# Two transformer layers written out in place of a loop, with the last weight splits and gating laid between residual sums

## The reference, cut to what matters

```python
for l in range(DEPTH):
    x = x + 0.5 * swiglu(rmsnorm(x, ffn1_norm[l]), ffn1_w_gate[l], ffn1_w_up[l], ffn1_w_down[l])
    h = rmsnorm(x, mix_norm[l])
    ... = jnp.split(h @ w_in[l], split_at, axis=-1)      # three kinds of attention
    x = x + o @ w_out[l]
    x = x + 0.5 * swiglu(rmsnorm(x, ffn2_norm[l]), ffn2_w_gate[l], ffn2_w_up[l], ffn2_w_down[l])
```

## Time and profile before

| | us |
|---|---|
| median of 3 runs | 3130.5 (3124.9 to 3131.53) |
| profiled execution | 3123.23 |
| its span | 3121.4 |
| PE busy | 2920.3 (94%) |
| DVE busy | 1825.3 (58%) |
| ACT busy | 1121.3 (36%) |

### The profile page before, as it was taken

How to read it: one execution, slowest core, us unless ns; L and a number is a source line. 1 busy time by engine, 2 the same in 40 slices (tenths; PEclk the granted TensorE clock), 3 DMA queues, 4 the chain that set the end, 5 groups by cost and what they waited for, 6 DMA issues and landing times.

```text
span 3121.4 us, 36929 instructions
## 1 busy us (share of the span) xinstructions
PE 2920.3 (94%) x13194; PEld 2256.0 (72%) x13194; DVE 1825.3 (58%) x2653; ACT 1121.3 (36%) x1638; POOL 212.4 (7%) x68
## 2 busy tenths in 40 slices
PE   5999999999999998999999999999998999878995
PEld 3888877566688877888777566688876767566774
DVE  4556553675555655565544674566556645469775
ACT  3211132467322223221131566312114333356664
POOL 0000000000000000000000000000000000037663
PEclk8999999999999999999999999999999989989998
DMA  7322332100232322232232000323214212368895
GB/s 161 108 94 84 102 76 67 31 1 25 89 110 84 108 81 95 81 108 94 79 87 52 21 1 24 121 81 108 94 40 108 79 41 81 142 236 315 322 331 195
DMA packets 234685, 324.56 MB, mean 104 GB/s; under 512 B 58720, under 2 KB 202088, under 8 KB 222144
## 3 DMA queue, kind: packets, MB, share of 16 engines
q1 hardware_dynamic: 228400, 309.88, 30.4%
q0 software_dynamic: 5584, 11.02, 1.3%
q10 hardware_dynamic: 576, 2.10, 0.2%
HBM read 317.20 MB, written 14.16 MB: 106 GB/s over the span
## 4 chain that ended last, share of the span: by engine, by line
PE 83%; DVE 4%; DMA 3%; issue 2%; ACT 2%; POOL 2%; DVEq 1%; SPq 1%; ACTq 0%; POOLq 0%
PE score L909 10%; PE score L911 10%; PE score L910 10%; PE acc L1271 8%; PE acc L962 6%; PE acc L940 5%; PE acc L942 5%; PE acc L941 5%; PE score L996 4%; PE acc L1017 4%; PE score L1444 3%; POOL xd_lo L2750 2%; PE acc L1444 2%; PE acc L954 2%; DMA weights<-in_ffn_w_gate 1%
## 5 line engine op out<-in xcount | busy, mean ns | idle before, releaser
L2066 DVE SCALAR_TENSOR_TENSOR x_T<-acc,x_T 128x512 f32<-128x512 f32 x352 | 242.4, 691 | 402.8 <-PE acc L942 402.4
L909 PE MATMUL score<-h_hi,gate_hi 128*128 128x512 f32 x704 | 277.7, 394 | 22.1 <-DVE h_lo L2019 14.1
L910 PE MATMUL score<-h_lo,gate_hi 128*128 128x512 f32 x704 | 275.9, 392 | 0.0
L911 PE MATMUL score<-h_hi,gate_lo 128*128 128x512 f32 x704 | 275.9, 392 | 0.0
L909 PE MATMUL score<-h_hi,up_hi 128*128 128x512 f32 x704 | 275.6, 391 | 0.0
L911 PE MATMUL score<-h_hi,up_lo 128*128 128x512 f32 x704 | 273.9, 389 | 0.0
L910 PE MATMUL score<-h_lo,up_hi 128*128 128x512 f32 x704 | 273.9, 389 | 0.0
L940 PE MATMUL acc<-hid_hi,down_hi 128*128 128x512 f32 x640 | 252.1, 394 | 17.9 <-DVE x_T L2066 17.9
L942 PE MATMUL acc<-hid_hi,down_lo 128*128 128x512 f32 x640 | 251.3, 393 | 0.0
L941 PE MATMUL acc<-hid_lo,down_hi 128*128 128x512 f32 x640 | 251.2, 392 | 0.0
L1620 ACT ACTIVATE exp_tile<-probs 128x512 f32<-128x512 f32 x88 | 50.8, 625 | 409.1 <-DVE probs L2041 409.1
(11 more groups left out here) (437 smaller groups left out, 6350.1 us busy)
## 6 DMA issues: line engine op xcount, KB each, us to landing
weights<-in_ffn_w_gate SPq DMA_DIRECT2D x44, 1024.0 KB, 5.3
weights<-in_ffn_w_up SPq DMA_DIRECT2D x44, 1024.0 KB, 5.4
weights<-in_ffn_w_down SPq DMA_DIRECT2D x44, 1024.0 KB, 5.5
arena<-in_expert_w_gate SPq DMA_DIRECT2D x32, 1024.0 KB, 6.5
arena<-in_expert_w_up SPq DMA_DIRECT2D x32, 1024.0 KB, 6.9
weights<-in_expert_w_down SPq DMA_DIRECT2D x30, 1024.0 KB, 5.9
weights<-in_w_in SPq DMA_DIRECT2D x23, 1024.0 KB, 5.3
weights<-in_w_out SPq DMA_DIRECT2D x8, 768.0 KB, 4.4
```

Source lines behind the costliest of these rows:

```text
L909: mm(ps, hi[:, kc, cols], h_hi[:, kc, :], start=kc == 0, stop=False, skip_group_check=True)
L910: mm(ps, hi[:, kc, cols], h_lo[:, kc, :], start=False, stop=False, skip_group_check=True)
L911: return mm(ps, lo[:, kc, cols], h_hi[:, kc, :], start=False, stop=kc == KC - 1, skip_group_check=True)
L2066: V.scalar_tensor_tensor(x_T[:, c, :], acc[c % 2][:, :], 0.25, x_T[:, c, :], ALU.mult, ALU.add).then_inc(acc_free[c % 2], 1)
```

## The change

It has four parts. (1) The loop over the two layers is written out on all four engines, so that the layer number is a constant; the last low halves of one feed-forward are joined to the next layer (`entering`). (2) At the end of a feed-forward DVE's work is laid out anew: after each of the eight sums of the last but one down product comes one part: for `ph` 1 two halves of the last down weights, then the three steps of `hidden`, then two halves of the next stage's first weights; for `ph` 0 the last down weights are split ahead of all sums, and ACT may split them as soon as the gate half of the last slice has been read. (3) Between the attention's output product and the second feed-forward, ACT splits the first gate weights after the first two chunks of x, and DVE in two halves after the sums of chunks 4 and 5. (4) With layer 1's first gate weights split there, the top of layer 1 has only the last low half left.

```diff
@@ sp, pe, act, dve: the layer loop @@
-            with dve.Fori(0, DEPTH) as l:
-                split_weights(l, 0, 0, 0)
-                for c in range(KC):
-                    low(l, 0, c)
+            for l in range(DEPTH):
+                if l == 0:
+                    split_weights(l, 0, 0, 0)
+                    for c in range(KC):
+                        low(l, 0, c)
+                else:
+                    low(l, 0, KC - 1)
                 add_squares(l * 3, ffn_sq, KC - 1)
...
@@ act @@
-            def enter(k, sq, hi):
+            def enter(k, sq, hi, first_gate=None):
 
                 for c in range(KC):
+                    if first_gate is not None and c == 2:
+                        split_weights(first_gate, 1, 0, 0)
...
-                act.wait_ge(gu_full, gu_at(l, gub, 2 * NSL))
+                act.wait_ge(gu_full, gu_at(l, gub, 2 * NSL - (1 if ph == 0 else 0)))
                 split_weights(l, ph, 2, NSL - 1, tile=ph)
...
                 slices(l, 0)
+                act.wait_ge(gu_full, gu_at(l, 0, 2 * NSL))
                 split_mix(l, 0)
                 enter(l * 3 + 1, mix_sq, mix_h[0])
                 mix(l)
-                split_weights(l, 1, 0, 0)
-                enter(l * 3 + 2, ffn_sq, h_hi)
+                enter(l * 3 + 2, ffn_sq, h_hi, first_gate=l)
                 slices(l, 1)
@@ dve @@
-            def split_weights(l, ph, w, sl, tile=None):
+            def split_weights(l, ph, w, sl, tile=None, half=None):
 
                 tile = w if tile is None else tile
+                cols = slice(0, 2048) if half is None else slice(1024 * half, 1024 * half + 1024)
                 dve.wait_ge(w_hi_ready[w], at(l, 2 * NSL, ph * NSL + sl + 1))
-                V.tensor_tensor(w_lo[tile][:, :], slot[w][:, :], w_hi[tile][:, :], ALU.subtract).then_inc(w_split[w], 1)
+                m = V.tensor_tensor(w_lo[tile][:, cols], slot[w][:, cols], w_hi[tile][:, cols], ALU.subtract)
+                if half != 0:
+                    m.then_inc(w_split[w], 1)
...
+                entering = (l, 1) if ph == 0 else (l + 1, 0) if l + 1 < DEPTH else None
...
                         if last:
                             dve.drain().then_inc(x_final, 1)
-                            if ph == 0 and c >= 1:
-                                low(l, 1, c - 1)
+                            if entering is not None and c >= 1:
+                                low(*entering, c - 1)
...
-                split_weights(l, ph, 2, NSL - 1, tile=ph)
-                down(NSL - 2, chunks=range(KC // 2))
-                hidden(NSL - 1, 0)
-                down(NSL - 2, chunks=range(KC // 2, KC))
-                if ph == 0:
-                    split_mix(l, 0)
+
+                def between(c):
+
+                    down(NSL - 2, chunks=(c,))
+                    if c < 2:
+                        if ph == 1:
+                            split_weights(l, ph, 2, NSL - 1, tile=ph, half=c)
+                    elif c < 5:
+                        hidden(NSL - 1, 0, (c - 2,))
+                    elif c < 7 and ph == 0:
+                        split_mix(l, 0, half=c - 5)
+                    elif c < 7 and l + 1 < DEPTH:
+                        split_weights(l + 1, 0, 0, 0, half=c - 5)
+
+                if ph == 0:
+                    split_weights(l, ph, 2, NSL - 1, tile=ph)
+                for c in range(KC):
+                    between(c)
                 down(NSL - 1, True)
...
                 add_out("p", 7)
-                split_weights(l, 1, 0, 0)
                 dve.drain()
                 for c in range(KC):
                     add_out("q", c)
                     dve.drain().then_inc(x_final, 1)
                     if c >= 1:
                         low(l, 2, c - 1)
+                    if c in (4, 5):
+                        split_weights(l, 1, 0, 0, half=c - 4)
```

More of the change, by code:

```diff
@@ L1239, in _ @@
                ).then_inc(rel_full, 1)
-            with pe.Fori(0, DEPTH) as l:
+            for l in range(DEPTH):
                 slices(l, 0)
@@ L1770, in _ @@
             act.wait_ge(x_final, KC)
-            with act.Fori(0, DEPTH) as l:
+            for l in range(DEPTH):
                 split_weights(l, 0, 0, 0)
@@ L2000, in square_sum, with split_mix @@
                         m.then_inc(summed, 1)
-            def split_weights(l, ph, w, sl, tile=None):
+            def split_weights(l, ph, w, sl, tile=None, half=None):
                 tile = w if tile is None else tile
+                cols = slice(0, 2048) if half is None else slice(1024 * half, 1024 * half + 1024)
                 dve.wait_ge(w_hi_ready[w], at(l, 2 * NSL, ph * NSL + sl + 1))
-                V.tensor_tensor(w_lo[tile][:, :], slot[w][:, :], w_hi[tile][:, :], ALU.subtract).then_inc(w_split[w], 1)
-            def split_mix(l, n):
+                m = V.tensor_tensor(w_lo[tile][:, cols], slot[w][:, cols], w_hi[tile][:, cols], ALU.subtract)
+                if half != 0:
+                    m.then_inc(w_split[w], 1)
+            def split_mix(l, n, half=None):
                 dve.wait_ge(mix_w_hi_ready, at(l, N_SPLIT, n + 1))
-                w = LOAD_COLS[n]
-                V.tensor_tensor(mix_w[n % 2][1][:, 0:w], slot[n % 3][:, 0:w], mix_w[n % 2][0][:, 0:w],
-                                ALU.subtract).then_inc(mix_w_split, 1)
+                cols = slice(0, LOAD_COLS[n]) if half is None else slice(1024 * half, 1024 * half + 1024)
+                m = V.tensor_tensor(mix_w[n % 2][1][:, cols], slot[n % 3][:, cols], mix_w[n % 2][0][:, cols],
+                                    ALU.subtract)
+                if half != 0:
+                    m.then_inc(mix_w_split, 1)
             def low(l, nth, c):
@@ L2049, in gate, with hidden @@
                         V.scalar_tensor_tensor(et[:, c, :], et[:, c, :], 1.0, gated2[c], ALU.add, ALU.mult)
[L2051 to L2061, removed]
+                def hidden(sl, par, parts=range(3)):
+                    for part in parts:
+                        dve.drain()
+                        if part == 0:
+                            dve.wait_ge(gu_full, gu_at(l, gub, sl * 2 + 2))
+                            for c in range(2):
+                                V.tensor_tensor(et[:, c, :], et[:, c, :], score[2 + c][:, :], ALU.mult)
+                        elif part == 1:
+                            V.tensor_copy(hid_hi[:, 2 * par:2 * par + 2, :], et[:, :, :])
+                        else:
+                            V.tensor_tensor(hid_lo[:, 2 * par:2 * par + 2, :], et[:, :, :],
+                                            hid_hi[:, 2 * par:2 * par + 2, :], ALU.subtract).then_inc(hid_done, 2)
+                entering = (l, 1) if ph == 0 else (l + 1, 0) if l + 1 < DEPTH else None
                 def down(sl, last=False, chunks=range(KC)):
```

1 line of the change is left out of this document (removed).

## The result

The kernel after takes 3072.4 us (median of four executions, 3070.8 to 3074.4), the one before 3129.1 (four executions): a ratio of 0.982, 95% interval 0.9803 to 0.9837. Five more executions of it gave 3072.6 and 0.9819 (0.9806 to 0.9832). So 56 us were won. The forecast was 3084 and its range began at 3073: the direction came out, and so did the time of each of the places A to D in the trace, but the saving in the medians was underrated. The two profiled executions differ by less than the medians: 3123.23 before and 3074.36 after, 48.9 (spans 3121.4 and 3072.4).

What follows compares the result with a forecast made beforehand. PE, busy 2920.3 of 3121.4 us, plus its gaps was taken as the bound. Savings 13.8 + 5.05 + 12.5 + 16.7 + 2 = 50, less 3.2 for the clock, 46.8; from median 3130.5 to 3084, range 3073 to 3099.

Steps and rivals of the forecast that it cites:

- A: First feed-forward to attention, twice: DVE work in pieces behind the sums starts attention 6.9 us earlier each, 13.8 in all.
- B: Attention to second feed-forward, twice: the gate product starts 8.3 us earlier each, 16.7 in all.
- C: Layer 0 to layer 1, once: no jump and no weights in front of the gate product, saving 12.5 us.
- D: Layer 1 to the second block, once: the last sum starts at 23.6 in place of 28.65, saving 5.05 us.
- signs of being wrong: PE waiting over 2 us at B, clock under 0.9 for longer after a down phase, or longer slices or attention.
- the base: Whole kernel: median 3130.5 lies 7.3 us above the profiled 3123.2; the same saving makes it 3083.7.
- The clock: Four down phases: many short waits keep some matmuls slow; half of 6.4 us, so 3.2, given back.
- Rival (1): Down phases: short waits keep the clock down and DVE pieces run longer; saving 38 us, time 3093; chance 0.14.
- What else moves: Mainly attention of both layers: written-out layers take register work out; bounds 0 and 19 us, 2 taken.
- Rival (2): Attention: half of 19 us of register work comes free and the clock stays up; saving 57, time 3074; chance 0.11.
- Rival (3): Longer straight-line code: PE stalls at instruction packets; at 1 us each 18 us slower, 3149; chance 0.03.
- Rival (4): At B the halves release nothing earlier, saving only 2.4 us of DVE's weights; saving 35, time 3096; chance 0.04.

Runs made afterwards that it cites:

- e2: Kernel before with the layer loop written out on all four engines, no instruction moved: 3114.1 us, ratio 0.9950; again 3117.3, 0.9963.
- e8: Kernel after with GpSimd's rel_scratch store held until about 580 us and ACT's table load made early by a one-column copy: 3062.5 us; again 3064.3.
- e9: Kernel after with only ACT's one-column copy ahead of its wait for x, so its table load comes early: 3076.7 us, ratio 0.9832.

## Why the prediction was wrong, and where it was right

**A, B, C, D: right.** In the two pairs of traces they won 13.5 and 13.8, 17.2 twice, 12.6 and 14.1, 5.0 and 5.1, for 13.8, 16.7, 12.5 and 5.05. Undone on the chip, B cost 18.1 and the ends 27.4. None of the signs of being wrong that the prediction names was seen.

**The step that failed: the base.** "The median of the runs shown, 3130.5, lies 7.3 above it; with the same saving it becomes 3083.7" took the 7.3 as something that both kernels have. Measured, the median of before is 5.4 above its profiled execution (3128.6 and 3123.2), and that of after 2.0 below its own (3072.4 and 3074.4). The forecast missed by 11.3, and that adds up: 7.3 carried over, 2.0 that after's median lies below its profile, and 2.1 that the two profiled executions are further apart (48.9) than the working says (46.8).

Why the 7.3 did not stay is in part shown. The profiled execution of before was one of its two fastest in 87. The second trace of before, nearer to the median, is 1.6 longer by the low clock at three places and 1.3 shorter at one; two of the three, A of layer 1 and the feed-forward behind C, have no low clock at all in after. With the second pair the saving is 54.7. On the side of after it was luck: both of its profiles were the slowest of their sets.

**The clock: wrong by all of its 3.2.** The prediction gave back half of 6.4 for many short waits. After has nine waits at L2077, 0.3 at the longest, and no low stretch at A, C or D, nor at B. So the term was 0, and without it the sum would have been 50 for the 48.9 of the first pair. The rule of the Trainium skill that was weighed there ("TensorE: Matmul & The Clock Gate", section "A second HAM failure mode: psum-queue depth-cycling") does not come true for waits as short as these. Rival (1) is out: the low clock did not stay, and A took 23.76 for the 23.5 laid out.

**The layers written out: the part that cannot be seen in one trace.** The working holds 3.15 for the jump, 2 in "What else moves", and about 1.2 at each A, where it puts 1.50 a chunk for 1.69: some 7.5 in all. At an equal clock 8 to 9 were measured, 3.2 of them at the jump and 1.2 at each A. So the work itself was sized well, though the 2 do not lie in attention, where I looked for them. In the medians the same edit gave 11.6 and 15.6. What is missing from the working is that its executions run more of the time at the full clock, which is worth 3 to 7. Rival (2), at 3074 the nearest to the result, was right that the clock stays up and wrong on the place: it took 9.5 from register work in attention, which lasts 382 with registers and without them.

From e2 to after 41.5 and 44.7 were measured. The steps left to it are A, D, C without the jump and B, 13.8 + 5.05 + 9.35 + 16.7, less the 2.4 at A that e2 has already: 42.5, with nothing given back for the clock.

**What stays open.** Why the low stretches come less often once DVE's loop is written out is not shown. Nor is where 2 to 3 of the 8 to 9 at an equal clock lie.

**Rival (3), code fetch: out.** The instruction queue q8 moved 61 packets, 1.00 MB, in after, for 65 and 1.06 MB, and the slices took 339.19 in place of 339.5. Rival (4) is out by B's 14.24. The table load at the start had not been foreseen, and no run shows that it costs the kernel anything.

## What to carry to other kernels

Lay a stage's end out on the two engines side by side, with the durations of the rows, and put one piece of work behind each release: this came out to 0.3 at all six places. Do not carry the distance between one profiled execution and the median over to the other kernel. It may hold just what the change removes, and the other profile has luck of its own, so the range must be widened by that distance on either side. A profile near the median, or a second one, is worth having before the forecast. And where the mean clock of every execution is known, compare executions at an equal clock: that parts the work that was saved from the clock that was won. A large store that nobody needs soon is to be moved to where the DMA engines rest, and not just away from where it hurts.

## What the runs showed of the hardware

- Behind two waits of 2.2 the granted clock fell to 0.57 over 4 us in one execution and stayed at 1.00 in another of the same kernel (A of layer 0 in the two traces of before); the price was 1.3 there and 1.6 at D. Behind the waits of 0.1 to 0.3 in the down phases it fell in none of five traces (after twice, e8 twice, e9).
- A loop's jump on DVE cost 3.1, and the register work ahead of a wait 0.18 for each low half (0.33 against 0.15).
- A store of 1.5 MB on GpSimd's queue held a load of 1 MB on SP's for up to 30 in place of 5.3, and the issue of another for 11.08 in place of 0.43. With the store moved to 567 us both were gone.
